# Attention scores of a one-core transformer kernel: four-pass float32 products replaced by single-pass products of rounded parts and remainders

## What is computed

```python
# first (a): 4 query heads on 2 key heads, all 768 keys, head size 128
q = apply_rope(rms_norm(heads(q, 4), q_g), cos, sin);  k likewise; kc = rms_norm(...)
s = einsum('bqhgd,bkhd->bhgqk', q, concat([kc, k])) * d ** -0.5;  p = softmax(s);  o = p @ v

# third (c): a window of 128 each side, plus the 256 context keys, a sink in the softmax
s_lat = where(valid, q @ kb.T * scale, -inf);  s_ctx = q @ kc.T * scale

# fourth (d): keys from a latent; 128 columns without and 64 with rotation
k = rms_norm(concat([ckv @ w_uk, broadcast(k_rope)]), k_g), last 64 columns rotated
s = q @ k.T * 192 ** -0.5
```

## Time and profile before

| what | us |
| --- | --- |
| median of three runs | 2757.79 |
| the profiled execution | 2757.12 |
| its span, first to last instruction | 2755.3 |
| TensorE busy | 2714.3 |
| attention a, units 0 to 15 | about 293 to 351 |
| attention c | about 757 to 805 |
| attention d | about 1061 to 1138 |

### The profile page before, as it was taken

One profiled execution on the slowest core, in us unless ns is written; L12 is line 12 of the kernel. 1 busy time (PEld: TensorE's weight loads), 2 busy tenths in 40 slices (PEclk: granted clock), 3 DMA queues, 4 the chain that ended last, 5 costly groups with the idle time before them and its releaser, 6 DMA issues.

```text
span 2755.3 us, 34390 instructions
## 1 busy us (share of the span) xinstructions
PE 2714.3 (99%) x13798; PEld 2152.6 (78%) x13798; DVE 1148.7 (42%) x1897; ACT 998.8 (36%) x1565; POOL 1209.6 (44%) x601
## 2 busy tenths in 40 slices
PE   7999999999999999999999999999999999999999
PEld 4578888888888776788876778677888887777887
DVE  3257343137540425222124577664223445666311
ACT  4343422342242334322223213564222335666311
POOL 1236035215603531355443335776655555445443
PEclk9999999999999999999999999999999999999999
DMA  9853443125682325133332333324443333222433
GB/s 368 313 174 107 108 123 90 46 82 191 187 119 70 92 61 153 39 115 115 100 93 77 92 92 86 98 77 136 125 119 96 92 92 108 77 77 77 149 115 88
DMA packets 450318, 318.20 MB, mean 115 GB/s; under 512 B 32337, under 2 KB 404817, under 8 KB 447345
## 3 DMA queue, kind: packets, MB, share of 16 engines
q1 hardware_dynamic: 418112, 280.03, 34.7%
q10 hardware_dynamic: 32048, 35.98, 5.3%
HBM read 299.08 MB, written 28.95 MB: 119 GB/s over the span
## 4 chain that ended last, share of the span: by engine, by line
PE 95%; DVE 1%; POOL 1%; issue 1%; ACT 1%; DMA 1%; SPq 1%; DVEq 0%; ACTq 0%; POOLq 0%
PE acc L2044 81%; PE aux L2044 7%; PE ssq L2047 3%; PE ssq L2044 2%; PE aux L2047 1%; POOL w_lo L1246 1%; DMA ada_ring<-in_w_ada 1%; DVE rstd L1544 0%; SPq L711 0%; ACT p_t L1069 0%; DVE p L1654 0%; ACT w_hi L950 0%; DVE gate_rows L1622 0%; POOL staged_lo L1263 0%; POOL sq_sum L1402 0%
## 5 line engine op out<-in xcount | busy, mean ns | idle before, releaser
L1246 POOL TENSOR_TENSOR w_lo<-raw,w_hi 128x1024 fp32r<-128x1024 f32 x362 | 878.1, 2426 | 1286.9 <-ACT w_hi L950 1286.9
L2044 PE MATMUL acc<-h_hi,w_hi 128*128 128x512 f32 (+1 forms) x3232 | 1194.0, 386 | 4.7 <-DVE h_lo L1470 1.4
L2044 PE MATMUL acc<-h_hi,w_lo 128*128 128x512 f32 (+1 forms) x3232 | 1172.5, 380 | 0.0
L2044 PE MATMUL acc<-h_lo,w_hi 128*128 128x512 f32 (+1 forms) x2464 | 872.3, 376 | 0.0
L950 ACT ACTIVATE w_hi<-raw 128x1024 fp32r<-128x1024 f32 x362 | 383.5, 1060 | 1027.2 <-PE acc L2044 1006.7
L2044 PEld LDWEIGHTS acc<-h_hi,w_hi 128*128 128x128 f32 x3232 | 584.2, 188 | 160.7 <-issue 46.0
L2044 PEld LDWEIGHTS acc<-h_hi,w_lo 128*128 128x128 f32 x3232 | 583.8, 188 | 118.5
L2044 PEld LDWEIGHTS acc<-h_lo,w_hi 128*128 128x128 f32 x2464 | 439.9, 188 | 82.4 <-issue 1.9
L2044 PE MATMUL acc<-out_t_lo,w_hi 128*128 128x512 f32 x768 | 299.1, 389 | 0.0
L1544 DVE RECIPROCAL rstd<-rstd 128x512 f32<-128x512 f32 (+1 forms) x29 | 118.0, 4070 | 271.2 <-ACT rstd L998 271.2
L2044 PEld LDWEIGHTS acc<-out_t_lo,w_hi 128*128 128x128 f32 x768 | 144.4, 188 | 28.9
(11 more groups left out here) (258 smaller groups left out, 2494.7 us busy)
## 6 DMA issues: line engine op xcount, KB each, us to landing
raw<-in_w_in SPq DMA_DIRECT2D x52, 1024.0 KB, 5.9
raw<-in_even_w_in SPq DMA_DIRECT2D x41, 1024.0 KB, 5.6
raw<-in_odd_w_in SPq DMA_DIRECT2D x36, 1024.0 KB, 5.6
ada_ring<-in_w_ada SPq DMA_DIRECT2D x32, 1024.0 KB, 5.9
gate_ring<-in_w_ada SPq DMA_DIRECT2D x16, 1024.0 KB, 5.8
raw<-in_w_out SPq DMA_DIRECT2D x16, 1024.0 KB, 5.9
raw<-in_even_w_out SPq DMA_DIRECT2D x16, 1024.0 KB, 5.8
raw<-in_odd_w_out SPq DMA_DIRECT2D x16, 1024.0 KB, 6.6
```

The source lines that it names most:

```text
L1246: G_.tensor_tensor(WL[half][:], RAW[G.rs][:, half * HALF * P:(half + 1) * HALF * P], WH[half][:].bitcast(F32), ALU.subtract).then_inc(S["l ...
L2044: return M.matmul(out_, lhsT, rhs, start=start, stop=stop, skip_group_check=True)
```

## The change

Scores in a and c are three single-pass products per piece: rounded q by rounded k, rounded q by k's remainder, q's remainder by rounded k. In d they are five: these three on the 128 unrotated columns, and two on a 128-row stack of the rotated 64 columns (rounded part and remainder of q one above the other) with the rounded part, and with the remainder, of k doubled. ACT makes the rounded parts (`split_hi`, `split_key`), POOL the remainders (`split_lo`, `split`), DVE the stacks (`dup_queries`, `dup_keys`). In c a piece of 384 now starts at column 128, so that the context is one piece of 256. Since the new tiles lie over others, some loads wait longer: the gate ring of b and the loads of x. The late rotation of the last key of d moves from vn[4] to vn[5]. In the silu group j = 8, `after(prev)` moves behind `dsa(1)`.

The diff, cut to its core, in the order plan (the first pair of `splits` is mixer c's, the second a's), SP, ACT (`split_hi`, called first in `chore`, then the step of vn[1]), POOL, DVE, TensorE:

```diff
+gs[10].splits, gs[11].splits = ("K0", "K1"), ("Q0", "Q1", "Q2", "Q3")
+gs[6].splits, gs[7].splits = ("Q0", "Q1", "Q2"), ("K0", "K1", "Q3")
-    vn[0].late_turn, vn[4].late_turn = kn[1], kn[3]
+    vn[1].chore, vn[3].chore, vn[5].chore = "split_first", "split_third", "split_last"
+    vn[0].late_turn, vn[5].late_turn = kn[1], kn[3]
...
+                    if g in (4, 5):
+                        sp.wait_ge(S["s_ready"], FIRST_U["b"])
-                        sp.wait_ge(S["half_done"], 2 * (G.g - 1))
+                        sp.wait_ge(S["s_ready"], FIRST_U["d"] + 16) if G.layer == 0 else sp.wait_ge(S["half_done"], 2 * (G.g - 1))
...
+                A.activation(high, of, ACT.Copy).then_inc(S["split_hi"], 1)
...
+                if G.chore == "split_first":
+                    need(act, "xn_done", G.queries[3].norm + 1)
+                    for h in range(4):
+                        A.activation(ktile(QHD, h, SEQ), ktile(Q, h, SEQ), ACT.Copy).then_inc(S["split_hi"], 1)
+                    for h in range(2):
+                        split_key(G.kn[h])
...
-                if G.kind == "kn" and G.j == 0:
-                    pool.wait_ge(S["half_done"], 2 * prev.g + 2)
-                    G_.memset(QRP[:], 0.0).then_inc(S["pad_clear"], 1)
+                for what in G.splits:
+                    split_lo(G, what)
                 if m == "d":
+                    for h in range(4):
+                        split(h, item["keys"])
+                    pool.wait_ge(S["split_lo"], SPLIT["d"] + 20)
                     for half in range(2):
                         lo(tail[0], half)
+                if s == 3:
+                    pool.wait_ge(S["normed"], 9)
...
+                if G.kind == "vn" and G.j == 0:
+                    dup_keys(0)
                 if G.kind == "kn" and G.j == 1:
-                    pad_queries()
+                    dup_queries(G)
                 norm(prev)
+                if G.kind == "vn" and G.j == 0:
+                    dup_keys(1)
+                    if m == "d" and n in (1, 2):
+                        dup_keys(n + 1)
-                    if scores_first:
-                        after(prev)
-                    for _, name, s in middle:
+                    for n, (_, name, s) in enumerate(middle):
                         unit[name](s)
+                        if scores_first and n == 0:
+                            after(prev)
...
-                settled(pe, item["total"], ("xn_done", "rope_done"))
+                settled(pe, item["total"], ("xn_done", "rope_done") if m != "d" else ("xn_done",))
-                    parts, at_ = [], 0
+                    parts, at_ = [], 512 - (hi_key - lo_key) if m == "c" and hi_key - lo_key > 256 else 0
+                    if m == "d" and qt == 0:
+                        pe.wait_ge(S["split_lo"], SPLIT["d"] + 5 * (h + 1))
+                    if m in "ac" and qt == 0:
+                        pe.wait_ge(S["split_lo"], max(split_count(m, f"Q{h}"), split_count(m, f"K{kv}")))
+                            mm(dst, qh[:, of], kh[:, key:key + w], True, False)
+                            mm(dst, qh[:, of], kl[:, key:key + w], False, False)
+                            e = mm(dst, ql[:, of], kh[:, key:key + w], False, True)
+                        mm(dst, QHD[:, of], KDH[:, at_key], True, False)
+                        mm(dst, QHD[:, of], KDL[:, at_key], False, False)
+                        mm(dst, QLD[:, of], KDH[:, at_key], False, False)
+                        mm(dst, QST[:, of], KRH[:, at_key], False, False)
+                        e = mm(dst, QST[:, of], KRL[:, at_key], False, True)
```

More of the change, by code:

```diff
@@ L297, in mixer @@
         gs += values()
+        for G in gs:
+            G.mixer, G.keys, G.queries = m, keys, [H for H in gs if H.dst == "Q"]
         if m == "a":
@@ L545, in build @@
             "std_done", "rs_done", "xn_done", "perm_done", "partner_done", "cos_done", "aux_free", "rope_done", "silu_done",
-            "copied", "fp32_done", "pad_clear", "pad_done", "dve_link", "pool_link",
+            "copied", "fp32_done", "split_hi", "dup_hi", "split_lo", "dve_link", "pool_link",
             "s_ready", "neg_ready", "p_ready", "t_ready", "pt_ready", "o_ready", "on_ready", "turned", "out_done",
@@ L1015, in _, with split_key @@
             step.eng = act
+            def split_key(K_):
+                need(act, "xn_done", K_.norm + 1)
+                A.activation(ktile(KDH, K_.j, TOK), ktile(KD, K_.j, TOK), ACT.Copy).then_inc(S["split_hi"], 1)
             def flush(prev, prev2):
@@ L1300, in step, with split_lo @@
                         add_columns(h)
+            def split_lo(G, what):
+                of, high, low = split_parts(G.mixer, what)
+                pool.wait_ge(S["split_hi"], split_count(G.mixer, what))
+                G_.tensor_tensor(low, of, high.bitcast(F32), ALU.subtract).then_inc(S["split_lo"], 1)
             def add_columns(h):
@@ L1325, in attend, with split @@
                 pool.wait_ge(S["out_done"], U0 + 16)
+            def split(h, kn):
+                own, other = ((0, 64), (64, 128))[::1 - 2 * (h % 2)]
+                own, other = slice(*own), slice(*other)
+                need(pool, "split_lo", SPLIT["d"] + 5 * h)
+                pool.wait_ge(S["split_hi"], SPLIT["d"] + h + 1)
+                G_.tensor_tensor(ktile(QLD, h, SEQ), ktile(Q, h, SEQ), ktile(QHD, h, SEQ).bitcast(F32),
+                                 ALU.subtract).then_inc(S["split_lo"], 1)
+                pool.wait_ge(S["dup_hi"], h + 1)
+                pool.wait_ge(S["split_lo"], SPLIT["d"] + 5 * h + 1)
+                G_.tensor_tensor(ktile(QST, h, SEQ)[other, :], ktile(QR, h // 2, SEQ)[own, :],
+                                 ktile(QST, h, SEQ)[own, :].bitcast(F32), ALU.subtract).then_inc(S["split_lo"], 1)
+                pool.wait_ge(S["split_hi"], SPLIT["d"] + 4 + h + 1)
+                pool.wait_ge(S["split_lo"], SPLIT["d"] + 5 * h + 2)
+                G_.tensor_tensor(ktile(KDL, h, TOK), ktile(KD, h, TOK), ktile(KDH, h, TOK).bitcast(F32),
+                                 ALU.subtract).then_inc(S["split_lo"], 1)
+                pool.wait_ge(S["dup_hi"], 4 + 2 * h + 2)
+                need(pool, "stage_used", kn[3].stage + 1)
+                if h:
+                    need(pool, "xn_done", kn[3].norm + 1)
+                for n, rows in enumerate((own, other)):
+                    pool.wait_ge(S["split_lo"], SPLIT["d"] + 5 * h + 3 + n)
+                    G_.tensor_tensor(ktile(KRL, h, TOK)[rows, :], ktile(KR, h // 2, TOK)[own, :],
+                                     ktile(KRH, h, TOK)[own, :].bitcast(F32), ALU.subtract).then_inc(S["split_lo"], 1)
             def pick(s):
@@ L1574, in norm, with dup_queries, dup_keys @@
                     e.then_inc(S["xn_done"], 1)
-            def pad_queries():
-                dve.wait_ge(S["pad_clear"], 1)
+            def dup_queries(G):
+                need(dve, "half_done", G.gates_read)
                 for h in range(4):
                     rows = slice(64 * (h % 2), 64 * (h % 2) + 64)
-                    Vv.tensor_copy(ktile(QRP, h, SEQ)[rows, :], ktile(QR, h // 2, SEQ)[rows, :])\
-                      .then_inc(S["pad_done"], 1)
+                    Vv.tensor_copy(ktile(QST, h, SEQ)[rows, :], ktile(QR, h // 2, SEQ)[rows, :])\
+                      .then_inc(S["dup_hi"], 1)
+            def dup_keys(h):
+                own = slice(64 * (h % 2), 64 * (h % 2) + 64)
+                for rows in (own, slice(64, 128) if h % 2 == 0 else slice(0, 64)):
+                    Vv.tensor_copy(ktile(KRH, h, TOK)[rows, :], ktile(KR, h // 2, TOK)[own, :])\
+                      .then_inc(S["dup_hi"], 1)
             def rotate(G):
```

55 lines of the change are left out of this document (47 added, 8 removed).

## The result

The changed kernel takes 2763.86 us (median of 18 runs, 2756.01 to 2765.74), the kernel before 2757.53: a ratio of 1.0019, 95% interval 1.0013 to 1.0026. It is 6 us slower where I had forecast 15 us faster. Within 2% it is no change, but the 21 us between forecast and result have places, and most of this part is about them. The ratios compare fast runs alone, so that two far slower ones, 4535.28 us of the kernel before and 10921.11 us of e3, do not count in them. The profiled execution took 2763.98, with a span of 2762.2 and a granted clock of 0.992, which was 0.997.

The account below looks back on a forecast made before the run. TensorE, busy 2714 of 2755 us, was taken as the bound. Terms -3.6 - 11.2 - 1.3 + 2.2 - 1.2 = -15.1 us on the profiled 2757.12 gave 2742.0, stated as 2742.5; the 8-in-10 range was 2737 to 2750.

Parts of the forecast that it names:

- attention a: Term for a: 0.25 us less per score for fourteen scores, plus 0.1; -3.6 us, bounds -2.5 and -4.
- attention d: Term for d: 0.85 us less per score, fourteen times, less 0.7 at the head; -11.2 us, bounds -9 and -12.
- attention c: Term for c: scores 0.2 us cheaper on average, half of it gained, fourteen times; -1.3 us, bounds 0 and -2.8.
- POOL ahead of c: Term before attention c: key remainders delay POOL's weight remainder and TensorE stands; +2.2 us, bounds 0.3 and 4.5.
- late part: Term around dsa(2): its 3.46 us wait goes, but later maxima come late; -1.2 us, bounds +1 and -5.
- rival C: Softmax chain bounds a and d as it does c, losing half of 3.5 + 11.9: 2750; chance 0.06.
- rival D: In a, c and d each new product waits for its weight load, +55 us against -15: 2797; chance 0.02.
- Here TensorE is not the limit: Step for attention c: TensorE's own work is 2.54 of 2.82 us, and the exponential waits 0.53 us for DVE's maximum.
- the half rule: Step for attention c: two periods are chain plus work, so half of what TensorE's work loses is gained, -1.3 us.
- alone they take 2 x 1.81 us: Step ahead of c: the undisturbed time of POOL's two key remainders, placed between the weight remainders.
- I charge 0.7: Step at the head of d: charge for DVE's last key rotation, possibly one or two us longer beside POOL.
- Rival B: New waits take more: loads of x 3, POOL in c 4.5, d's first maximum 2 us late: 2749; chance 0.14.

Follow-up runs that it names:

- e3: Changed kernel with d's second pair of key copies moved from ahead of the last rotation to behind the second maximum: 2759.72 us, 1.0004 of the kernel before.
- e4: Changed kernel with all six of a's remainders behind the last weight remainder, none of queries beside the gate sums: 2759.57 us, 1.0007 of the kernel before.
- e2: Changed kernel with c's two key remainders on POOL behind both weight remainders of the last silu group: 2750.39 us, 0.9978 of the kernel before.
- e5: Changed kernel with DVE's old order in silu group j = 8, reciprocal and scaling ahead of dsa(1)'s maxima: 2766.84 us, 1.0027 of the kernel before.
- e1: Changed kernel with the 6 MB write of swa_bias_dram issued behind attention c instead of at its head: 2787.03 us, 1.0110 of the kernel before.
- e10: Changed kernel with the 6 MB write of swa_bias_dram issued at the head of attention b instead of c: 2798.75 us, 1.0152 of the kernel before.
- e9: Changed kernel with attention c's scores as plain float32 products again and c's remainders gone: 2746.92 us, 0.9956 of the kernel before.
- c2: Changed kernel with the edits of e9, e3 and e4 together, the write left in c: 2740.39 us, 0.9939 of the kernel before.
- e7: Changed kernel with c's quarters 1 and 2 cut into 384, 128 and 128 columns, nine single-pass products: 2758.61 us, 0.9997 of the kernel before.

## Why the prediction was wrong, point by point

The shifts of the first table, against the terms of the sum:

| term | forecast | measured | where it was measured |
| --- | --- | --- | --- |
| attention a | -3.6 | -3.5 | shift over the attention |
| gate fold of a | no term | +2.6 | wait; gone in e4 |
| attention d | -11.2 | -6.7 | units -10.4, head +3.7 |
| attention c | -1.3 | +7.8 | about: stands 6.4, clock 2.5, units -0.8 |
| POOL ahead of c | +2.2 | +6.2 | wait 4.2, slow stretch behind it 1.7 to 1.8; gone in e2 |
| late part | -1.2 | 0.0 | shift over the group; e5 |
| kernel's start and mixer b | no term | +0.6 | not of the change |
| sum | -15.1 | +7.0 | span +6.9 |

The measured 2763.86 lies outside the range of 2737 to 2750, and one of the signs of being wrong came true: a clock below 1.00 inside an attention.

**Right: the price of the products, in a and d.** Units shorter by 0.24 and 0.82 us; rival C, that the copies and maxima would bound them, is out. So is rival D. The trace has the new products 0.23 and 0.12 us apart with a full-row weight load each, so the load costs nothing that can be seen. D's 55 us were also counted too high: of the 352 new products only 80 are added records (13878 against 13798), since each float32 product was two records with a load each. By the Trainium skill ("TensorE: Matmul & The Clock Gate", The mechanism), in the sentence that I had gone by, a load overlaps only where the row group differs, and D would have held; the trace disagrees. The same section also lets a load into the background weight buffer go ahead, which I had left out; no run here shows which buffer a load uses.

**Wrong: attention c, 9 of the 22 us.** The step that failed is "Here TensorE is not the limit", followed by a sum of the engines alone: -1.3 us, with nothing for the 6 MB write. Measured: +7.8. I had looked at four engines and not at the queues that bring TensorE's own instructions, though a window of the kernel before would have shown them full from 781 on (1.03). The new scores then use up TensorE's instructions sooner than the next packet comes. e1 and e10 show that without the write the stands go, e9 that without the new scores they go too. The term itself was half right in size: with the write elsewhere (e1) eleven periods take 806.02 - 775.79 = 30.23 us, where they took 799.15 - 768.31 = 30.84:

```profile
775.79 0.28 PE L2157 MATMUL aux<-ident_sb,o_nat 128*128 128x128 f32 x1
...
806.02 0.27 PE L2157 MATMUL aux<-ident_sb,o_nat 128*128 128x128 f32 x1
```

```profile
768.31 0.27 PE L2047 MATMUL aux<-ident_sb,o_nat 128*128 128x128 f32 x1
...
799.15 0.27 PE L2047 MATMUL aux<-ident_sb,o_nat 128*128 128x128 f32 x1
```

That is 0.055 us a unit, 0.8 in all, for the 1.3 that the half rule gave.

**Wrong size: POOL ahead of c, 4 us.** The place and the mechanism were right; the step "alone they take 2 x 1.81 us" was not, because they were not alone. I charged DVE's gate sums to the weight remainder and not to the key remainders in the same stretch, which took 3.89 and 3.85 us, so the end came at 752.46, past my bound of 751.9. And the half clock behind a stand was named ("may run slowly for a while") but got no price. By the Trainium skill ("GPSIMD Engine Reference", Specifications) the two engines contend for SBUF interfaces when DVE's instruction has two SBUF inputs. The trace agrees: 3.85 us against 1.82 beside such sums, and in the head of d the one instruction of the rotation with a single SBUF input kept its 0.69 us. Priced at the slowed rate of the earlier trace rows, 4.17 for 2.4, the two key remainders would have ended at 749.1 and the weight remainder at 751.5, still a microsecond short of 752.46, for they were slowed 2.1 times.

**Missing: the gate fold of a, 2.6 us.** I priced POOL's additions in c and d and wrote nothing about those in a, which stand beside the same kind of gate sums. It is the same mechanism at a third place.

**Wrong size: the head of d, 3 of the 4.5 us.** "Beside POOL it may take one or two us longer. I charge 0.7" was the step. It cost 3.77 us of wait and a clock of 0.50 behind it. Two instructions of 0.69 became 1.72 and 2.19, which is 2.5 us. The rotation also started 0.4 us late (1.12 us behind the start of the product that it waits for, 0.70 in e3), since the second pair of copies stood ahead of it, the first of them 2.17 us long beside POOL and the second 0.56. "DVE's four pairs of copies fall where it waits" did not hold for this pair.

**Nothing instead of 1.2 us: the late part.** The wait moved from dsa(2) to dsa(3) and shrank from 3.46 to 2.33 us, as reasoned. But behind the new stand the half clock lasted until about 1767, some 6 us, where it had been 4. A stand's price is the stand and the slow stretch behind it, and a shorter stand need not have a shorter one.

Rival B, the new waits at their upper ends, was the right kind, at 2749; two of its three places were met, and it stopped at 7 us for all of them. The loads of x cost nothing, as forecast: TensorE has no wait from 1146 to 1313.

## What to carry to other kernels

When work is given to an idle engine, list what the neighbouring engine does in the same microseconds and price both at the slowed rate, at every place the change touches and not only where it looks tight. Then add to each stand of TensorE the slow stretch behind it. Where a long DMA fills the queues, ask who else uses them, TensorE's own instructions and everything issued later on the same queue included; here 6 MB hidden under an attention left the next 256 instructions in time when they followed 18.1 us of work, and not when they followed 16.1.

## What the runs showed that I had not expected

- TensorE's instructions arrive in packets of 16 KB, 256 at a time, every 25 us or so all through the run, and full DMA queues can make them late: stands of 0.3 to 5.0 us in all seven traces that have both the write and the new scores of c, and none inside attention c, behind its first transposes, in the six that lack one of the two. The Trainium skill ("Trainium Architecture — The Big Picture", The software stack) tells of instruction streams being moved at load time; the traces show instruction packets moved during the run too, 111 of them on q8.
- These stands may be what makes the times vary: the runs of c2 span 2.3 us, those of e2 14. That is not shown, since only one run of each has a trace, and the runs of the kernel before, whose trace has no such stand, span 7.4.
- A DMA issue can hold its engine: 22.27 and 14.76 us on ACT, 10.59 on SP, behind a write of 6 MB; in the changed kernel the same issues of ACT took 0.58 and 0.68.
- A single-pass product of 128 columns costs 0.11 us in e7, as much as one of 256.
